# Handing out a bitwise key search on VectorE in two portions per attention unit, and its tie ranking in three pieces

## The chip, the cores and the metric

One core of one Trainium2 chip. The metric is the device time of the kernel in microseconds, median of the runs. Engines: PE is TensorE, DVE is VectorE, ACT is ScalarE, POOL is GpSimd, SP issues the DMAs. Each engine runs its own list of instructions in order, and waits on semaphores for the others.

## The reference

Two transformer blocks in float32, 1024 tokens, width 1024. What matters here is the first block. Its attention has two halves: a dilated window attention (8 heads), and an attention in which each query sees only its top 256 keys by an index score.

```python
q_pos = start + jnp.arange(BLOCK)
causal = key_pos[None, :] <= q_pos[:, None]
dots = jnp.einsum('bqhd,bsd->bqhs', qi_blk, ki).astype(jnp.float32)
score = jnp.einsum('bqh,bqhs->bqs', wi_blk.astype(jnp.float32), jax.nn.relu(dots)) * IDX_SCALE
score = jnp.where(causal[None], score, -jnp.inf)
_, sel = lax.top_k(score, topk)
...
s = jnp.where(valid[:, None], s, -jnp.inf)
p = jax.nn.softmax(s, axis=-1)
return jnp.einsum('bhqk,bqkd->bqhd', p.astype(v.dtype), v_sel)
```

The rest of the first block (gates, output projection, a gated feed-forward part of 2816) and the second block (two kinds of attention, a feed-forward part of 4096) are not touched.

## The kernel before, in words

The kernel first writes a list of stages, `S`, in Python. Every engine's program goes through the same list and emits its own instructions of each stage. So the order of the list is the order on every engine, and a stage that only one engine has (such as `topk`, on DVE alone) takes its place in that engine's queue.

**Units.** Attention of the first block goes by units (phase, head pair c, tile i). Phase a is the dilated half: c = 0 to 3, and for each the tiles i = 0 to 7 of 128 queries. Phase b is the sparse half: the tiles from 0 to 7, and for each the four pairs. Below, a(1,7) is pair 1, tile 7. A unit of tile i has 128 (i + 1) keys, for two heads. For tiles 4 to 7 its scores are made in two passes of at most 512 keys; each pass has a PSUM buffer `big` (there are two). `take` on PE gives a pass the buffer that the woven weight product doesn't hold, and waits until its previous content has been read.

The stages of a unit:

- `sc`: PE multiplies queries and keys (L1090); DVE reads the result with bias and minimum into `prob` (L2123); ACT is left the exponentials (L1430), whose sums go to `sm`.
- `nm`: DVE takes the reciprocals `rc` of the two sums (L2134); ACT scales both rows with them (L1424).
- `pv`: PE transposes the probabilities (L1113), ACT copies them out of PSUM (`pt`, L1384), PE multiplies them with the values (L1128). ACT does the next unit's two exponentials between these copies.
- `oc`: DVE copies the result to `y_a` or `y_b` (L2157).

`attend` runs them with one unit ahead: in step n it puts nm(n), then pv(n-1), sc(n+1), oc(n-1), and then `topk` with the portion of unit n. Between them `weave` puts pieces of weight products on PE (L924): projections in phase a, 16 gates in phase b. For a gate ACT reads PSUM (L1456) and POOL multiplies `gst_b` (L2490); POOL also splits the weights (`w_lo`, L2400) and in phase a rotates queries and keys (L2457, L2460, L2464).

**The search.** The 256th largest index score of each query is found bit by bit, for the tiles 2 to 7 in three batches, (2, 3, 4), (5, 6) and (7). For each of 32 bits there is a *count* per tile (L2059: how many scores reach `edge`) and one *step* per batch (L2065 makes `flip`, L2070 changes `edge`). When a batch is through, each of its tiles has a *rank* piece of seven operations (L2080 to L2093) that writes the mask over the index scores `idx_acc`. All run on DVE. The mask of a tile is wanted by the first b unit of that tile.

Each piece has a planned cost (a count P(i+1)/960 + 0.2, a step 0.75, a ranking 5P(i+1)/960 + 1.2). `spread(s)` is a unit's portion, `share` times its planned PE time; `topk(budget)` adds it to a credit (at most 12) and takes pieces while the credit is more than half the cost of the next one. So what is left over counts in the next call.

Of the kernel before, what the change touches and what calls it, by code (L numbers as in the profile page):

```python
# [22 lines left out]
P = 128  # L23
# [90 lines left out]
def _emit(nc, ctx, known, a):  # L114
    base0 = (nc.sbuf_base + 63) // 64 * 64

    def at(name, offset, shape, dt=F32):
        return nc.alloc_sbuf_tensor_at(name, shape, dt, offset=base0 + offset)
# [26 lines left out]
    edge, above = at("edge", M0 + 7168, [P, QT]), at("above", M0 + 7200, [P, QT])  # L145
# [7 lines left out]
    rot1, rot2 = at("rot1", R0 + 8 * K, [P, T]), at("rot2", R0 + 12 * K, [P, T])  # L153
# [14 lines left out]
    acc_at = [sum(P * (j + 1) for j in range(i)) for i in range(QT + 1)]  # L168
    acc = at("idx_acc", G2 + 46 * K, [P, acc_at[QT]])
# [261 lines left out]
    batches = [(2, 3, 4), (5, 6), (7,)]  # L431
    search = []
    counts = []
    for tiles in batches:
        for bit in range(31, -1, -1):
            counts += [(P * (i + 1) / 960 + 0.2, "count", bit, i, tiles) for i in tiles]
            counts.append((0.75, "step", bit, tiles))
    ranks = [[(5 * P * (i + 1) / 960 + 1.2, "rank", i, tiles) for i in tiles] for tiles in batches]
    credit, share = [0.0], [0.0]

    def take_pieces(wanted):

        n0 = len(search)
        while counts and wanted():
            search.append(counts.pop(0)[1:])
        if len(search) > n0:
            add("topk", n0, len(search))

    def topk(budget):

        def wanted():
            if credit[0] <= counts[0][0] / 2:
                return False
            credit[0] -= counts[0][0]
            return True

        credit[0] = min(credit[0] + budget, 12.0)
        take_pieces(wanted)
# [45 lines left out]
    def attend(units, filler, late, before=None):  # L504

        if before:
            before(units[0])
        add("sc", units[0], 0)
        for n, s in enumerate(units):
            weave_in(filler.get(n, []))  # L510
            add("nm", s, 0)
            if n:
                add("pv", units[n - 1], 0)
                add("pv", units[n - 1], 1)
                weave(group_points(units[n - 1]))
            if n + 1 < len(units):
                if before:
                    before(units[n + 1])
                add("sc", units[n + 1], 0)
            if n:  # L520
                add("oc", units[n - 1])
            if n + 1 < len(units):
                weave(score_points(units[n + 1]))
            for f in late.get(n, []):
                add(*f)
            topk(spread(s))
        return units[-1]

    def attend_pairs(units, filler, early, late):

        add("sc", *units[0])
        for n, (s, ti) in enumerate(units):
            weave_in(filler.get(n, []))
            if n >= 2 and ti == 0 and s[0] == "m":
                add("pt", units[n - 1][0])
            if n + 1 < len(units):
                add("sc", *units[n + 1])
                weave(2)
            for f in early.get(n, []):
                add(*f)  # L540
            add("nm", s, ti)
            if n >= 2:
                old = units[n - 2 + (ti == 0)][0]
                add("pv", old, ti)
                if ti:
                    add("oc", old)
                weave(3 if ti == 0 else 1)
            elif woven:
                add("ahead", 3)
                weave(3)  # L550
            for f in late.get(n, []):
                add(*f)
        return units[-1][0]

    def last_product(s):

# [4 lines left out]
    def spread(s):  # L561

        return share[0] * (0.75 * (s[2] + 1) + 1.36 * (score_points(s) + group_points(s)))
# [22 lines left out]
    for tiles, after in zip(batches[1:], ranks[1:]):  # L586
        n = 1 + max(n for n, x in enumerate(counts) if x[1:] == ("step", 0, tiles))
# [97 lines left out]
    order = []  # L685
# [1126 lines left out]
    def _(dve):  # L1812
# [88 lines left out]
        for stage, *x in S:  # L1901
# [66 lines left out]
            elif stage == "lin" and x[0][:2] != "va":  # L1968
                name, = x
                kind, c = name[:2], name[2:]  # L1970
# [12 lines left out]
            elif stage == "cnorm":  # L1983
                n = {"cq0": 0, "cq1": 1, "ckv": 2}[x[0]]
# [25 lines left out]
            elif stage == "idx":  # L2010
                c, = x
                dve.wait_ge(*s_te.at("t", "wi", 0))
                for hh in range(2):
                    for i in range(2, QT):
# [3 lines left out]
                        z = acc[:, acc_at[i]:acc_at[i + 1]]  # L2018
# [8 lines left out]
            elif stage == "iparts":  # L2027
                c, = x
# [8 lines left out]
            elif stage == "fill":  # L2037
# [4 lines left out]
                for i in range(2, QT):  # L2042
                    z = acc[:, acc_at[i + 1] - P:acc_at[i + 1]]
# [5 lines left out]
            elif stage == "topk":  # L2049
# [3 lines left out]
                for n in range(x[0], x[1]):  # L2053
                    kind, *what = search[n]
                    if kind == "count":
                        bit, i, tiles = what
                        z, tally = acc[:, acc_at[i]:acc_at[i + 1]], (rot1 if n >= late_pieces else tally_a)[:, 0:P * (i + 1)]
                        dve.wait_ge(s_tk.sem, s_tk.count)
                        dve.tensor_scalar(tally, z, edge[:, i:i + 1], 0.0, ALU.is_ge, ALU.add,  # L2059
                                          accum_out=above[:, i:i + 1]).then_inc(*s_tk.mark("count", bit, i))  # L2060
                    elif kind == "step":
                        bit, tiles = what
                        t = slice(tiles[0], tiles[-1] + 1)
                        dve.wait_ge(*s_tk.at("count", bit, tiles[-1]))
                        dve.tensor_scalar(flip[:, t], above[:, t], TOPK - 0.5, float(2 ** bit) if bit < 31 else -1.0, ALU.is_lt,  # L2065
                                          ALU.mult).then_inc(*s_tk.mark("flip", bit, tiles))
                        dve.wait_ge(*s_tk.at("flip", bit, tiles))
                        e = edge[:, t].bitcast(I32)
                        if bit:
                            ins = dve.scalar_tensor_tensor(out=e, in0=flip[:, t], scalar=2 ** (bit - 1), in1=e, op0=ALU.bitwise_xor,  # L2070
                                                           op1=ALU.bitwise_xor)
                        else:
                            ins = dve.tensor_tensor(e, flip[:, t], e, ALU.bitwise_xor)
                        ins.then_inc(*s_tk.mark("step", bit, tiles))
                    else:
                        i, tiles = what
                        z, e = acc[:, acc_at[i]:acc_at[i + 1]], edge[:, i:i + 1]
                        tie, order = rot1[:, 0:P * (i + 1)], rot2[:, 0:P * (i + 1)]
                        dve.wait_ge(s_tk.sem, s_tk.count)
                        dve.tensor_scalar(tie, z, e, 0.0, ALU.is_gt, ALU.add, accum_out=above[:, i:i + 1]).then_inc(*s_tk.mark("above", i))  # L2080
                        dve.wait_ge(*s_tk.at("above", i))
                        dve.tensor_scalar(spare[:, i:i + 1], above[:, i:i + 1], -1.0, float(TOPK), ALU.mult, ALU.add).then_inc(*s_tk.mark("spare", i))
                        dve.tensor_scalar(tie, z, e, None, ALU.is_equal).then_inc(*s_tk.mark("tie", i))
                        dve.wait_ge(*s_tk.at("tie", i))
                        dve.tensor_tensor_scan(order, tie, tie, 0.0, ALU.add, ALU.max).then_inc(*s_tk.mark("order", i))
                        dve.wait_ge(*s_tk.at("order", i))
                        dve.scalar_tensor_tensor(out=tie, in0=order, scalar=spare[:, i:i + 1], in1=tie, op0=ALU.is_gt,
                                                 op1=ALU.mult).then_inc(*s_tk.mark("late", i))
                        dve.wait_ge(*s_tk.at("late", i))
                        dve.scalar_tensor_tensor(out=tie, in0=z, scalar=e, in1=tie, op0=ALU.is_lt,  # L2090
                                                 op1=ALU.add).then_inc(*s_tk.mark("out", i))
                        dve.wait_ge(*s_tk.at("out", i))
                        dve.tensor_scalar(z, tie, MASKED, None, ALU.mult).then_inc(*s_tk.mark("mask", i))  # L2093
                        dve.wait_ge(*s_tk.at("mask", i))
            elif stage == "sc":
                s, ti = x
                st = step_of(s)
                n = nstep[s]
# [11 lines left out]
                for part, (k0, k1) in enumerate(spans):  # L2110
# [4 lines left out]
                    for at_, (lane, i, m) in enumerate(lanes(st, ti)):  # L2115
                        p = st["prob"][m][n % 2][:, lane, k0:k1]
                        c = 4 * (n % 2) + 2 * lane + m
# [8 lines left out]
            elif stage == "nm":  # L2126
                s, unit = x
                st = step_of(s)
                n = nstep[s]
                maps = st["n_maps"]  # L2130
                if st["heads"]:
                    c = 4 * (n % 2)
# [3 lines left out]
                for ti, i, _ in lanes(st, unit)[0:1]:  # L2136
                    nk = keys(st, i)
                    c = 4 * (n % 2) + 2 * ti
# [11 lines left out]
            elif stage == "oc":  # L2150
                s, = x
# [195 lines left out]
            elif stage in ("dnorm", "donorm"):  # L2347
                if stage == "dnorm":
                    which, h = x
                    key, gain, z = ("dnorm", which, h), which, (dqb if which == "dq" else dkb)[h % 2][:, :]  # L2350
                    out = (which, h)
                else:
                    h, = x
                    key, gain, z, out = ("donorm", h), "dout", yd[:, h, :], ("do", h)
# [12 lines left out]
            elif stage == "mn2":  # L2367
# [12 lines left out]
                z = (qz if which == "q" else kz)[h][:, :]  # L2380
# [488 lines left out]
```

## Time and profile before

| | us |
|---|---|
| median of 3 runs | 3199.21 |
| lowest, highest | 3197.5, 3201.7 |
| the profiled execution, its time | 3197.21 |
| its span | 3195.4 |
| PE busy over the span | 2968.6 (93%) |
| DVE busy over the span | 1757.7 (55%) |

Durations and spans below are those of the profiled execution. The attention units and the search lie between 194 and 840 us: phase a until 492, then some projections, phase b from 520. In the rows, times are us from the start of the span, "[x <-Y]" is how long the engine had been idle and whom it waited for, and "mn_part" is the minimum that DVE writes while it reads the first of two passes.

### The profile page before, as it was taken

To read this page: it belongs to the slowest core of one execution; us is meant where nothing else is said; L and a number is where in the kernel's file an instruction comes from. 1 tells how busy PE (TensorE), PEld (TensorE's weight loads), DVE (VectorE), ACT (ScalarE), POOL (GpSimd) and SP (SyncE) were. 2 spreads that over 40 slices of the span, in tenths; PEclk is the share of its full clock that TensorE was granted. 3 is DMA by queue.
4 is the path that set the end of the run, shared out by engine and by line. 5 is a ranking of instruction groups with operands and counts; after the bars stand their busy time and mean duration, and the time that the engine had idled before them with its cause. 6 is when DMAs were issued, how large, how long until landed. Compare 5 with 4: busy or idle time off the path is not lost. (4 is left out here: it accounts for less than half of the span.)

```text
span 3195.4 us, 36533 instructions
## 1 busy us (share of the span) xinstructions
PE 2968.6 (93%) x13886; PEld 2291.0 (72%) x13886; DVE 1757.7 (55%) x2633; ACT 1218.3 (38%) x1810; POOL 1251.4 (39%) x698
## 2 busy tenths in 40 slices
PE   7899887899999999999998899987889999999999
PEld 5666655666778788887886566655777788878887
DVE  4777776775232644445684554575453554455544
ACT  3455543554433433333133344455453322222110
POOL 4324324122244887773246110031002697732221
PEclk8999998999999999999999999998999999999999
DMA  6322111111251223324221311010002233342322
GB/s 176 84 54 60 47 45 48 40 54 44 80 187 52 67 83 92 82 79 138 66 90 35 110 39 33 14 40 17 10 4 89 67 108 105 118 159 92 101 76 73
DMA packets 279311, 236.37 MB, mean 74 GB/s; under 512 B 23748, under 2 KB 251972, under 8 KB 278596
## 3 DMA queue, kind: packets, MB, share of 16 engines
q1 hardware_dynamic: 279176, 234.65, 24.7%
q8 instruction: 75, 1.23, 0.2%
q14 instruction: 60, 0.49, 0.1%
HBM read 171.14 MB, written 53.51 MB: 70 GB/s over the span
## 5 line engine op out<-in xcount | busy, mean ns | idle before, releaser
L924 PE MATMUL big<-g_hi,w_hi 128*128 128x512 f32 x2112 | 693.2, 410 | 40.0 <-POOL w_lo L2400 16.5
L2400 POOL TENSOR_TENSOR w_lo<-w_raw,w_hi 128x1024 fp32r<-128x1024 f32 x147 | 357.2, 2430 | 927.5 <-ACT w_hi L1347 927.5
L924 PE MATMUL big<-g_lo,w_hi 128*128 128x512 f32 x2112 | 662.8, 395 | 0.0
L924 PE MATMUL big<-g_hi,w_lo 128*128 128x512 f32 x2112 | 659.9, 394 | 0.0
L924 PEld LDWEIGHTS big<-g_hi,w_hi 128*128 128x128 f32 x2112 | 381.8, 191 | 197.6 <-issue 121.8
L924 PEld LDWEIGHTS big<-g_lo,w_hi 128*128 128x128 f32 x2112 | 402.0, 191 | 88.4
L924 PEld LDWEIGHTS big<-g_hi,w_lo 128*128 128x128 f32 x2112 | 401.1, 190 | 87.9
L1347 ACT ACTIVATE w_hi<-w_raw 128x1024 fp32r<-128x1024 f32 x147 | 154.7, 1053 | 394.5 <-PE big L924 377.4
L1375 ACT ACTIVATE a_hi<-a_raw 128x512 fp32r<-128x512 f32 x114 | 72.1, 633 | 338.0 <-POOL a_raw L2407 338.0
L1196 PE MATMUL big<-b_hi,a_hi 128*128 128x512 f32 x456 | 178.5, 391 | 8.0 <-DVE b_lo L2204 6.1
L1196 PE MATMUL big<-b_hi,a_lo 128*128 128x512 f32 x456 | 178.1, 391 | 0.0
L1196 PE MATMUL big<-b_lo,a_hi 128*128 128x512 f32 x456 | 178.0, 390 | 0.0
L2415 POOL TENSOR_TENSOR a_lo<-a_raw,a_hi 128x512 fp32r<-128x512 f32 x114 | 153.7, 1348 | 31.9 <-ACT a_hi L1375 31.9
L2216 DVE TENSOR_TENSOR c<-c,big 128x512 f32<-128x512 f32 x114 | 78.3, 687 | 151.4 <-PE big L1196 150.0
L2216 DVE TENSOR_TENSOR c<-c,obank 128x512 f32<-128x512 f32 x76 | 52.2, 687 | 190.0 <-ACT c L1621 180.5
L1384 ACT ACTIVATE pt<-tbank 128x512 f32<-128x512 f32 (+1 forms) x160 | 84.0, 553 | 181.4 <-PE tbank L1113 181.2
L2490 POOL TENSOR_TENSOR gst_b<-gst_b,r_rep 128x1024 f32<-128x1024 f32 x16 | 38.4, 2402 | 243.7 <-ACT gst_b L1456 243.7
L2059 DVE TENSOR_SCALAR_CACHE_REDUCE tally_a<-idx_acc,edge 128x384 f32<-128x384 f32 (+2 forms) x147 | 126.6, 861 | 5.2
L1196 PE MATMUL tbank<-b_hi,a_hi 128*128 128x512 f32 x304 | 119.3, 392 | 4.2 <-POOL a_lo L2415 4.2
L1113 PE MATMUL tbank<-ident_sb,prob 128*128 128x128 f32 x576 | 88.5, 294 | 36.8 <-ACT prob L1424 34.6
L1424 ACT ACTIVATE prob<-prob,rc 128x256 f32<-128x256 f32 (+7 forms) x128 | 92.2, 769 | 79.2 <-DVE rc L2134 79.1
L1196 PE MATMUL tbank<-b_lo,a_hi 128*128 128x512 f32 x304 | 118.3, 389 | 0.0
(337 smaller groups left out, 5570.5 us busy)
## 6 DMA issues: line engine op xcount, KB each, us to landing
a_spill<-c SPq DMA_DIRECT2D x54, 512.0 KB, 3.3
g_lo<-a_spill SPq DMA_DIRECT2D x54, 512.0 KB, 5.1
w_raw<-in_w_in SPq DMA_DIRECT2D x51, 512.0 KB, 4.3
w_raw<-in_w_down SPq DMA_DIRECT2D x40, 512.0 KB, 4.3
w_raw<-in_w_up SPq DMA_DIRECT2D x27, 512.0 KB, 6.0
u_raw<-in_w_up SPq DMA_DIRECT2D x27, 512.0 KB, 6.0
rot<-rope_in SPq DMA_DIRECT2D x68, 128.0 KB, 2.3
g_spill<-gst_b SPq DMA_DIRECT2D x16, 512.0 KB, 3.0
```

The source lines that it names most:

```text
L924: ins = pe.matmul(out[0:m, HALF * h:HALF * h + HALF], w[slot][:, col:col + m], x[:, HALF * h:HALF * h + HALF], start=p == 0, stop=p == tot ...
L1113: ins = pe.transpose(tbank[tn[0] % 2][:, o:o + P], st["prob"][0][n % 2][:, ti, P * kt:P * kt + P], ident[:, :])
L1196: ins = pe.matmul(banks[q], w[q][:, P * k:P * k + P], x[q][:, k, :], start=(k == 0 and z == 0), stop=(k == 3 and z == 2))
L1347: act.activation(w_hi[w % 2][:, :], w_raw[w % 2][:, :], ACT.Copy).then_inc(*s_whi.mark(w))
L1375: act.activation(ah[q][:, :], az[q][:, :] if src is None else src, ACT.Copy).then_inc(*s_ah.mark(stage, q, n))
L1384: act.activation(dest, src, ACT.Copy).then_inc(*s_te.mark(*key))
L1424: act.activation(p, p, ACT.Copy, scale=rc[:, c:c + 1]).then_inc(*s_nrm.mark(s, lane))
L2059: dve.tensor_scalar(tally, z, edge[:, i:i + 1], 0.0, ALU.is_ge, ALU.add, accum_out=above[:, i:i + 1]).then_inc(*s_tk.mark("count", bit, i))
L2216: dve.tensor_tensor(dest, one_, banks[other] if isinstance(other, int) else other, op).then_inc(*s_dr.mark(stage, m, what))
L2400: pool.tensor_tensor(w_lo[s][:, :], w_raw[s][:, :], w_hi[s][:, :].bitcast(F32), ALU.subtract).then_inc(*s_wlo.mark(w))
L2415: pool.tensor_tensor(al[q][:, :], az[q][:, :] if src is None else src, ah[q][:, :].bitcast(F32), ALU.subtract).then_inc(*s_al.mark(stage, ...
L2490: pool.tensor_tensor(z[:, :], z[:, :], r_rep[:, :], ALU.mult).then_inc(*s_gt.mark(name))
```

## The change

In `attend`, the portion of a unit is handed out in two calls. The first comes where the whole one was (behind sc(n+1) and oc(n-1)), and has at most what the two exponentials of the next unit take by a formula, `exponentials`. The rest comes behind the next unit's nm, and so ahead of sc(n+2). The ranking of a tile becomes three pieces, `ties` (three operations), `order` (the scan) and `rank` (the remaining three), which are handed out one by one; their planned costs add up to 6P(i+1)/960 + 1.2.

```diff
-    ranks = [[(5 * P * (i + 1) / 960 + 1.2, "rank", i, tiles) for i in tiles] for tiles in batches]
+    ranks = [[(c * P * (i + 1) / 960 + 0.4, kind, i, tiles) for i in tiles for c, kind in ((1.7, "ties"), (1.8, "order"), (2.5, "rank"))]
+             for tiles in batches]
...
+        rest = 0.0
         add("sc", units[0], 0)
         for n, s in enumerate(units):
             weave_in(filler.get(n, []))
             add("nm", s, 0)
+            topk(rest)
             if n:
                 add("pv", units[n - 1], 0)
...
-            topk(spread(s))
+            first = min(spread(s), exponentials(units[n + 1])) if n + 1 < len(units) else spread(s)
+            rest = spread(s) - first
+            topk(first)
         return units[-1]
...
+    def exponentials(s):
+
+        return 2 * (P * (s[2] + 1) / 960 + 0.25)
...
-                    else:
+                    elif kind == "ties":
                         i, tiles = what
...
                         dve.tensor_scalar(tie, z, e, None, ALU.is_equal).then_inc(*s_tk.mark("tie", i))
+                    elif kind == "order":
+                        i, tiles = what
+                        tie, order = rot1[:, 0:P * (i + 1)], rot2[:, 0:P * (i + 1)]
                         dve.wait_ge(*s_tk.at("tie", i))
                         dve.tensor_tensor_scan(order, tie, tie, 0.0, ALU.add, ALU.max).then_inc(*s_tk.mark("order", i))
+                    else:
+                        i, tiles = what
+                        z, e = acc[:, acc_at[i]:acc_at[i + 1]], edge[:, i:i + 1]
+                        tie, order = rot1[:, 0:P * (i + 1)], rot2[:, 0:P * (i + 1)]
                         dve.wait_ge(*s_tk.at("order", i))
```

## Rows read from the trace of the kernel before

**Rows 1.** Busy time of each engine in three stretches, then PE clock and DMA.

```profile
core 0: us, PE busy (x) PEld busy (x) DVE busy (x) ACT busy (x) POOL busy (x), PEclk, DMA share, GB/s
194.00:482.00 288.00, 260.16 (x1584) 182.37 (x1584) 222.39 (x646) 153.69 (x293) 91.78 (x39) 0.96 0.19 50
482.00:540.00 58.00, 43.46 (x227) 33.64 (x228) 37.58 (x85) 17.92 (x37) 26.88 (x12) 0.85 0.16 38
540.00:840.00 300.00, 279.29 (x1666) 195.64 (x1665) 179.65 (x478) 154.03 (x280) 65.90 (x28) 0.98 0.16 48
```

**Rows 2.** Waits of PE, ACT and DVE, 194 to 840: total us, times, longest.

```profile
PE tbank L1113 <- ACT prob L1424: 34.6, 15, 5.7
PE big L1090 <- DVE mn_part L2123: 9.2, 6, 3.9
...
PE big L1090 <- POOL qb L2464: 5.2, 1, 5.2
...
ACT prob L1424 <- DVE rc L2134: 79.1, 42, 11.2
...
DVE prob L2123 <- PE big L1090: 100.1, 74, 3.8
DVE rc L2134 <- ACT prob L1430: 62.6, 27, 8.4
```

**Rows 3.** Timeline of unit b(2,5): start, duration, instruction, idle before.

```profile
699.53 1.28 DVE L2059 TENSOR_SCALAR_CACHE_REDUCE rot<-idx_acc,edge 128x1024 f32<-128x1024 f32 x1
...
701.04 0.16 DVE L2070 SCALAR_TENSOR_TENSOR edge<-flip,edge 128x1 int32<-128x1 int32 x1
701.24 1.28 DVE L2059 TENSOR_SCALAR_CACHE_REDUCE rot<-idx_acc,edge 128x1024 f32<-128x1024 f32 x1
...
704.01 0.93 ACT L1430 ACTIVATE prob<-prob,mn 128x768 f32<-128x768 f32 x1
...
704.76 1.13 PE L1090 MATMUL big<-kb_b,qb 64*128 64x512 f32 x4
...
705.06 0.17 DVE L2134 RECIPROCAL rc<-sm 128x2 f32<-128x2 f32 x1 [0.46 <-ACT prob L1430]
...
706.02 2.40 POOL L2490 TENSOR_TENSOR gst_b<-gst_b,r_rep 128x1024 f32<-128x1024 f32 x1 [17.43 <-ACT gst_b L1456]
706.04 0.69 DVE L2123 CUSTOM_DVE_ANT_0 prob<-big,idx_acc 128x512 f32<-128x512 f32 x1 [0.81 <-PE big L1090]
...
707.27 0.08 DVE L2123 DVE_READ_ACCUMULATOR2_ANT mn_part<- 128x1 f32 x1
...
707.65 0.70 PE L1090 MATMUL big<-kb_b,qb 64*128 64x256 f32 x4
```

**Rows 4.** Timeline around 748, POOL and DVE.

```profile
748.12 2.40 POOL L2490 TENSOR_TENSOR gst_b<-gst_b,r_rep 128x1024 f32<-128x1024 f32 x1 [14.18 <-ACT gst_b L1456]
...
748.66 1.88 DVE L2070 SCALAR_TENSOR_TENSOR edge<-flip,edge 128x1 int32<-128x1 int32 x1
```

**Rows 5.** Timeline of unit a(1,7).

```profile
326.85 0.19 ACT L1430 ACTIVATION_READ_ACCUMULATOR prob<-prob,mn 128x1 f32 x1
...
331.41 0.16 DVE L2134 RECIPROCAL rc<-sm 128x2 f32<-128x2 f32 x1
...
333.89 1.51 PE L1113 MATMUL tbank<-ident_sb,prob 128*128 128x128 f32 x6 [5.67 <-ACT prob L1424]
```

**Rows 6.** Timeline behind the ranking of tile 7.

```profile
760.98 0.69 DVE L2123 CUSTOM_DVE_ANT_0 prob<-big,idx_acc 128x512 f32<-128x512 f32 x1
...
762.35 0.92 PE L1090 MATMUL big<-kb_b,qb 64*128 64x384 f32 x4 [3.70 <-DVE mn_part L2123]
```

**Rows 7.** Short stretches, columns as in rows 1.

```profile
334.00:337.00 3.00, 3.00 (x12) 2.77 (x13) 2.93 (x5) 2.31 (x5) 2.18 (x1) 0.55 0.00 0
...
257.00:260.00 3.00, 0.83 (x8) 0.67 (x9) 2.34 (x10) 3.00 (x4) 2.37 (x1) 1.00 0.00 0
...
480.00:484.00 4.00, 3.99 (x27) 3.40 (x28) 3.88 (x11) 2.32 (x4) 3.35 (x2) 0.57 0.53 135
...
763.00:767.00 4.00, 4.00 (x15) 3.12 (x14) 1.65 (x6) 0.12 (x1) 0.00 (x0) 0.57 0.00 0
```

## The prediction

> **What bounds the kernel now.** I read the stretch table first. The change acts only from 194 to 840 us, where the attention units and the search run; outside it the order of work is the same. In that stretch PE is busy 260 of 288 us, 43 of 58 and 279 of 300, DVE 222, 38 and 180 [rows 1], so PE is the bound with DVE close behind it in the first half. Then the waits: PE stands 34.6 us, 15 times, for scaled probabilities (ACT prob) and 9.2 us, 6 times, for the first pass of scores being read out of PSUM (DVE mn_part); ACT stands 79.1 us for reciprocals, while DVE stands 62.6 us in front of reciprocals whose exponentials are not done, and 100.1 us in front of score reads whose matmuls are not done [rows 2]. So both directions occur: in some units the search makes the reciprocal late, in others DVE has time to spare.
>
> The timeline of one late unit shows the fault that the edit can mend. The last exponential of unit a(1,7) (phase, head pair, tile) ends at 327.0, but DVE goes on with its portion and divides at 331.41; PE's next transposes wait 5.67 us [rows 5]. The timeline of a usual large unit, b(2,5), shows the other side: the second exponential starts at 704.01 and is done, its sum read, just ahead of the reciprocal at 705.06, PE's first pass of the next scores runs from 704.76 to 705.9, DVE reads it from 706.04 to 707.35, and PE's second pass starts at 707.65 [rows 3]. That second pass takes the PSUM buffer of the first (the other one is held by the woven weight product), so it can't start before the read: 0.3 us of slack, and in most such units under 0.1.
>
> **The change, part by part.** *The split.* A unit's portion is `spread`; the first part becomes what two exponentials take in the planner's formula, 1.6 to 2.6 us for units before tiles 3 to 7 and 0.8 us before tile 0. With share 0.56 the portion is 6 to 8 us for tiles 4 to 7 (0.56 x (0.75 x 6 + 1.36 x 5) = 6.3 for tile 5), so some 4 to 5 us become the remainder, issued behind the next reciprocal and ahead of the next scores. Pieces are whole, and in fact faster than planned: in b a count and its step take 699.53 to 701.24, 1.71 us [rows 3], against 2.02. Counting pieces against the credit gives remainders of 3.1 to 3.9 us in a's tiles 5 and 6, 4.8 to 5.1 in its tile 7, and 2.1 to 4.8 in b's tiles 4 to 6, mostly two counts with their steps (3.4). Tiles below 4 get 0.4 to 2.5.
>
> *What the exponentials really cost.* ACT does the second exponential behind a PSUM read that waits for PE's transposes: the exponentials of b(2,5) are done 5.5 us after DVE's portion starts at 699.53 [rows 3]. In the large units whose portion now just fits, DVE will therefore idle 2 to 3 us ahead of the reciprocal and do the remainder after it.
>
> *The price.* The first score read moves from its present start to the end of the exponentials + 0.2 + remainder. In b(2,5) two counts and two steps give 705.0 + 0.2 + 3.4 = 708.6 instead of 706.04: 2.6 us late, less 0.3 of slack, 2.3 us of PE standing. That such lateness is PE's one to one shows behind the largest ranking: scores read late at 760.98, second pass waits 3.70 [rows 6]. It does not wear off over the units, since each unit's exponentials are tied to PE's own progress. By this sum for each unit, 17 units with a two-pass successor pay: a's tiles 4 to 6 (seven of them) 12 us together, b's tiles 3 to 6 (ten) 18 us: 30 us. Small units have one pass and keep 1 us or more until their transposes: nothing, from 0 to 3 together. Behind tile 7 of a (6.5 us of pieces ahead of the scores of tile 1) the read is 3 us late, covered by the transposes of tile 0; uncovered it would be 3 x 3.
>
> *POOL.* The step's small operation on `edge` takes 0.16 us [rows 3], but 1.88 when it falls in a POOL operation: 748.66 + 1.88 = 750.54, the end of POOL's 748.12 + 2.40 [rows 4]. POOL's gate product starts at 706.02, 0.96 us behind the reciprocal [rows 3], just where the remainder will be, while now the score reads lie there and are not held. A step at 706.9 would wait until 708.4. That hits every second b unit (b(2,4), b(0,5), b(2,5), b(0,6)) for 1.2 to 2.5 us, and in a five units whose rotation runs on POOL: full count 15 us. Where steps fall will shift, so I take half, 8, and keep 0 and 15.
> The Trainium skill, GPSIMD Engine Reference, section 1 (Specifications), says that POOL's SBUF interfaces are shared with VectorE and that instructions with two SBUF inputs or in a 2-port mode contend. The trace agrees, 0.16 against 1.88.
>
> *The gain.* Where the reciprocal was late and PE waited, it comes at the end of the exponentials: PE gets back the smaller of the two. Ten of the 15 waits qualify, for 25 us (from 0.3 at 256.5 to 4.9 at 622.3); one is 4.4 of the 5.67 [rows 5]. Two of these lose 2 to 3.5 us to their own predecessor's remainder, and 1 goes to POOL: 18 stay. The late score reads give 5 of their 9.2 (of the 3.70 about 2, for the ties and order pieces now lie behind the reciprocal) [rows 2, 6]. Gain 23.
>
> *Clock.* After the 5.67 us wait the granted clock is 0.55 over 334 to 337, after a 2.34 us wait 0.57 over 480 to 484, after the 3.70 one 0.57 over 763 to 767, but after a 2.17 us wait 1.00 [rows 7]: the lower level is 1.2 of 2.4 GHz, a half. These rows cost 3 x 0.45 = 1.4 and 4 x 0.43 = 1.7 us; over the nine such stretches between 334 and 767 it is about 2 each. Seven go with their waits (-13), and eight or nine come where the new waits exceed 3 us if POOL holds them up fully (+17), two or three if not (+5). From +4 to -9; I take -3.
>
> *Ranking in three pieces* adds no instruction, and moves them; the planner's total for rankings rises from 5 to 6 units a column, so DVE does about three pieces more before b starts, covered by the wait for the rotated queries (5.2 us on PE [rows 2]), behind which the ties of tile 2 stand too.
>
> Sum: 30 + 8 - 23 - 3 = +12, 30 + 15 - 23 + 4 = +26 with all holds and the clock that goes with them, and 30 - 23 - 9 = -2 without holds. Holds look regular in b, so I go above the middle: +17 on the profiled execution's 3197.2 (span 3195.4), that is 3214. That execution lies 2.0 below the median of the three runs, so the median after is 3216.
>
> **Rivals.**
> 1. *The remainder is hidden* (faster). PE's second pass doesn't suffer, because the read gets done under the woven product. It decides at a mean stall of (23 + 9) / 17 = 1.9 us per unit without holds; at half my stalls, 15, the sum is 15 - 23 - 9 = -17: 3182. For it: 62.6 us of DVE idle before reciprocals are still there and 100.1 before score reads [rows 2]. Against: slack under 0.1 us in front of the second pass, and [rows 6].
> 2. *A wash.* No holds at POOL and no new clock losses: -2, 3197; within 0.2%.
> 3. *POOL holds every step that meets it*, at either end of the remainder: +26 or more, 3225 to 3234. For it: the held step [rows 4] and POOL's place behind the reciprocal [rows 3]. The Trainium skill, GPSIMD Engine Reference, section 1, would have it so.
> 4. *The edit does little*, since credit carries over and whole pieces blur the split. Against: the portion exceeds the exponentials in every unit of both phases. 3199.
> The Trainium skill, TensorE: Matmul & The Clock Gate, Part 1, says that recent activity sets the clock and the throttled state is the default. By that rule the removed long waits return clock and the new short ones may not cost any, rival 2's side; the rows show both outcomes at 2.17 and 2.34 us.
>
> **How the numbers follow.** Forecast (3206 to 3224) 0.45; rival 3, 0.25; rivals 2 and 4, 0.17; rival 1, 0.13. The range 3192 to 3232 leaves 0.1 on each side or less; the forecast's own is 3206 to 3224. A measurement of this kernel tells about 0.2% (6.4 us) from no change: faster 0.13, same 0.17, slower 0.70.
>
> **What would show it.** Right: PE's wait for ACT prob falls from 34.6 to about 13, its wait for DVE mn_part rises from 9.2 to 35 or more, in some 17 portions of 1 to 5 us; DVE idles more than 62.6 us before reciprocals and far less than 100.1 before score reads; PE's busy time in 194 to 840 is nearly unchanged; steps of about 2 us behind reciprocals in b. Wrong, if mn_part stays under 20, or if the second passes wait and the unit still keeps its length, which would mean that PE had slack in these units that I did not see.

## The result, and the profile after

| | before, us | after, us |
|---|---|---|
| median | 3198.88 (4 runs, 3197.5 to 3201.7) | 3237.26 (4 runs, 3235.05 to 3242.92) |
| span of the profiled execution | 3195.4 | 3233.3 |
| first score matmul of phase a to last copy to `y_b` | 666.7 (195.0 to 861.7) | 701.0 (195.3 to 896.3) |
| PE busy over the span | 2968.6 | 2986.5 |

The ratio is 1.0122 [1.0104, 1.0139]: slower by 1.2%, where 3216 (3192 to 3232) was forecast. Of the 37.9 us that the profiled execution's span grew, 34.3 lie between the first scores of phase a and the end of phase b; I call this stretch the attention below. The page's head:

```profile
span 3233.3 us, 36529 instructions
PE 2986.5 (92%) x13886; PEld 2302.1 (71%) x13886; DVE 1746.2 (54%) x2633; ACT 1219.2 (38%) x1810; POOL 1250.0 (39%) x698
```

The waits of PE, ACT and DVE, 194 to 875 us of the kernel after (engine, line, whom it waited for: total us, times, longest), against [rows 2]:

```profile
DVE rc L2150 <- ACT prob L1439: 158.3, 51, 7.9
DVE prob L2139 <- PE big L1099: 50.7, 48, 3.5
PE big L1099 <- DVE mn_part L2139: 46.4, 19, 4.4
ACT prob L1433 <- DVE rc L2150: 17.5, 37, 6.5
ACT prob L1439 <- DVE mn L2139: 15.1, 10, 3.4
PE obank L1137 <- ACT pt L1393: 15.4, 17, 3.6
PE tbank L1122 <- ACT prob L1433: 10.6, 9, 3.2
PE big L1099 <- POOL qb L2480: 3.4, 1, 3.4
```

The rows show an exchange. The reciprocal isn't late any more: ACT waits for it 17.5 us instead of 79.1, and DVE stands 158.3 us in front of reciprocals instead of 62.6. PE gets back 24.0 us of its wait for scaled probabilities. What DVE no longer does before the reciprocal it does before the score read: its idle time there falls from 100.1 to 50.7, and PE's second pass waits 46.4 us, 19 times, instead of 9.2. Over the whole attention all listed waits of PE grow from 64.0 to 83.1 us, by 19.1: +37.2 for `mn_part`, -24.0 for ACT prob, +6.9 for `pt` (9.5 before, 16.4 after), and -1.0 for the others. That is half of the 37.9.

The three longest waits for `pt` (3.59, 2.45 and 2.13 us) come from the late score reads too, by way of ACT. ACT stands 15.1 us for the minimum `mn` of the finished scores, in front of its exponentials; before it was little:

```profile
ACT prob L1430 <- DVE mn L2123: 1.3, 2, 0.7
```

The longest of the three, with the copy of `pt` queued on ACT behind such an exponential (in front of the other two ACT stood 2.23 and 1.91 us for `mn`):

```profile
342.34 1.15 ACT L1439 ACTIVATE prob<-prob,mn 128x1024 f32<-128x1024 f32 x1 [3.37 <-DVE mn L2139]
...
343.49 0.58 ACT L1393 ACTIVATE pt<-tbank 128x512 f32<-128x512 f32 x1
...
344.12 1.12 PE L1137 MATMUL obank<-pt,va 128*64 128x128 f32 x8 [3.59 <-ACT pt L1393]
```

The other half is in the busy time. The same stretches as [rows 1] (busy us and instructions of PE, PEld, DVE, ACT, POOL, then PE clock, DMA share, GB/s):

```profile
core 0: us, PE busy (x) PEld busy (x) DVE busy (x) ACT busy (x) POOL busy (x), PEclk, DMA share, GB/s
194.00:508.00 314.00, 273.39 (x1615) 190.27 (x1615) 219.20 (x659) 157.98 (x300) 94.98 (x41) 0.93 0.18 46
508.00:560.00 52.00, 41.14 (x199) 31.79 (x198) 32.76 (x78) 14.48 (x32) 23.40 (x10) 0.86 0.17 41
560.00:875.00 315.00, 284.19 (x1666) 199.68 (x1665) 177.43 (x474) 153.96 (x277) 67.56 (x28) 0.96 0.15 46
```

PE does the same matmuls (3480 records against 3477), but is busy 598.7 us with them instead of 582.9, and its clock in phase a is 0.93 instead of 0.96. To size this I cut the trace into windows of half a us and summed PE busy x (1 - granted clock) from 197 us to the last copy to `y_b`: before 18.5 us in 9 stretches at the lower level, after 35.0 us in 17. So 19.1 of waits and 16.5 of clock make 35.6, against the 34.3 by which the attention grew. Where the clock fell:

```profile
254.00:258.00 4.00, 3.98 (x9) 2.09 (x10) 1.84 (x6) 0.00 (x0) 0.00 (x0) 0.50 0.17 53
...
705.00:709.00 4.00, 4.00 (x16) 3.37 (x16) 2.82 (x10) 0.94 (x2) 0.23 (x1) 0.58 0.50 138
736.00:740.00 4.00, 4.00 (x16) 3.42 (x15) 2.49 (x8) 1.33 (x3) 0.00 (x0) 0.57 0.10 29
...
722.00:725.00 3.00, 3.00 (x19) 2.58 (x18) 2.69 (x10) 1.30 (x3) 0.00 (x0) 1.00 0.00 0
```

These stand behind waits for `mn_part` of 4.4, 2.1, 3.5 and (the last row) 3.1 us. In the first three rows (0.50 to 0.58) PE is busy all the time, and its instructions take nearly twice as long, as the transposes below show.

The unit of [rows 3], b(2,5), in the kernel after:

```profile
728.35 1.13 PE L1099 MATMUL big<-kb_b,qb 64*128 64x512 f32 x4
728.66 0.17 DVE L2150 RECIPROCAL rc<-sm 128x2 f32<-128x2 f32 x1 [3.86 <-ACT prob L1439]
728.91 0.16 DVE L2079 SCALAR_TENSOR_TENSOR edge<-flip,edge 128x1 int32<-128x1 int32 x1
729.11 1.28 DVE L2068 TENSOR_SCALAR_CACHE_REDUCE rot<-idx_acc,edge 128x1024 f32<-128x1024 f32 x1
729.62 2.39 POOL L2506 TENSOR_TENSOR gst_b<-gst_b,r_rep 128x1024 f32<-128x1024 f32 x1 [24.39 <-ACT gst_b L1465]
730.62 1.42 DVE L2079 SCALAR_TENSOR_TENSOR edge<-flip,edge 128x1 int32<-128x1 int32 x1
732.07 1.28 DVE L2068 TENSOR_SCALAR_CACHE_REDUCE rot<-idx_acc,edge 128x1024 f32<-128x1024 f32 x1
733.39 0.69 DVE L2139 CUSTOM_DVE_ANT_0 prob<-big,idx_acc 128x512 f32<-128x512 f32 x1
734.61 0.08 DVE L2139 DVE_READ_ACCUMULATOR2_ANT mn_part<- 128x1 f32 x1
734.75 0.70 PE L1099 MATMUL big<-kb_b,qb 64*128 64x256 f32 x4 [3.46 <-DVE mn_part L2139]
737.33 1.91 PE L1122 MATMUL tbank<-ident_sb,prob 128*128 128x128 f32 x8
```

Everything of the forecast stands here in order. DVE idles 3.86 us for the sums, then does two steps and two counts. The second step takes 1.42 us instead of 0.16, because it meets POOL's gate product (729.62 + 2.39 = 732.01; 730.62 + 1.42 = 732.04). The score read comes 4.73 us behind the reciprocal instead of 0.98, the second pass waits 3.46 us, and the eight transposes behind it take 1.91 us at half the clock. In the kernel before they took 1.04:

```profile
709.77 1.04 PE L1113 MATMUL tbank<-ident_sb,prob 128*128 128x128 f32 x8
```

### The profile page after: what moved, and what is told of

Read it like the earlier page. It is cut to its first block and busy times, and to the rows that moved or that the text cites. A ratio compares the mean times of both kernels' runs of the same rounds, so it can differ in the third digit from the quotient of the medians.

```text
span 3233.3 us, 36529 instructions
## 1 busy us (share of the span) xinstructions
PE 2986.5 (92%) x13886; PEld 2302.1 (71%) x13886; DVE 1746.2 (54%) x2633; ACT 1219.2 (38%) x1810; POOL 1250.0 (39%) x698
## 5 line engine op out<-in xcount | busy, mean ns | idle before, releaser
L2431 POOL TENSOR_TENSOR a_lo<-a_raw,a_hi 128x512 fp32r<-128x512 f32 x114 | 153.3, 1345 | 31.9 <-ACT a_hi L1384 31.9
L1205 PE MATMUL tbank<-b_hi,a_lo 128*128 128x512 f32 x304 | 118.9, 391 | 0.0
L1205 PE MATMUL obank<-b_hi,a_hi 128*128 128x512 f32 x304 | 118.3, 389 | 0.0
```

The lines of the kernel that those rows point to most:

```text
L1205: ins = pe.matmul(banks[q], w[q][:, P * k:P * k + P], x[q][:, k, :], start=(k == 0 and z == 0), stop=(k == 3 and z == 2))
L2431: pool.tensor_tensor(al[q][:, :], az[q][:, :] if src is None else src, ah[q][:, :].bitcast(F32), ALU.subtract).then_inc(*s_al.mark(stage, ...
```

## The experiments

"Attention" is the stretch defined above, in the profiled execution; ratios are to the kernel before on the same chip, whose median was 3203.53 (e1 to e4), 3204.45 (e5 to e8) and 3203.06 (e9 to e12). "Waits" are PE's for `mn_part` / ACT prob; "lost" is the sum of PE busy x (1 - clock), as above, from 197 us to the last copy to `y_b` (in e1, whose attention starts at 200.5, 1.0 of it lies ahead). Attention, waits and lost are those of one execution each, the ratio is from all runs. The parts outside the attention, where nothing was changed, differ by up to 5.5 us each between executions, so the ratio and the attention say more than the span.

| run | ratio [95%] | span | attention | waits, us | lost, us |
|---|---|---|---|---|---|
| before | | 3195.4 | 666.7 | 9.2 / 34.6 | 18.5 |
| after | 1.0122 [1.0104, 1.0139] | 3233.3 | 701.0 | 46.4 / 10.6 | 35.0 |
| e1_ranks_only | 0.9929 [0.991, 0.9948] | 3189.9 | 650.5 | 7.6 / 21.6 | 19.8 |
| e2_split_only | 1.0159 [1.0134, 1.0183] | 3242.4 | 710.3 | 49.7 / 9.7 | 31.9 |
| e3_cap15 | 0.9931 [0.9912, 0.995] | 3178.9 | 646.0 | 9.6 / 17.4 | 14.9 |
| e12_cap30 | 1.0061 [1.0044, 1.0079] | 3222.0 | 689.3 | 37.1 / 13.5 | 30.7 |
| e4_small_gates | 1.0072 [1.0047, 1.0097] | 3227.1 | 694.4 | 40.5 / 10.9 | 34.2 |
| e8_before_small_gates | 0.9979 [0.9967, 0.9991] | 3192.6 | 664.3 | 7.5 / 31.8 | 23.1 |
| e5_pad2 | 1.0054 [1.0037, 1.0071] | 3215.5 | 683.9 | 23.3 / 34.7 | 21.2 |
| e6_pad4 | 1.0224 [1.0207, 1.0241] | 3276.8 | 743.6 | 59.4 / 32.8 | 48.5 |
| e7_weave2 | 1.0025 [1.0016, 1.0035] | 3202.2 | 672.3 | 18.0 / 9.7 | 23.4 |
| e9_cap15_weave2 | 0.994 [0.9926, 0.9955] | 3185.6 | 652.7 | 5.5 / 15.7 | 17.8 |
| e10_ranks_only_weave2 | 0.9967 [0.9954, 0.998] | 3190.3 | 661.8 | 5.4 / 20.6 | 18.3 |
| e11_before_weave2 | 1.0027 [1.0016, 1.0038] | 3211.0 | 680.3 | 8.2 / 31.9 | 24.2 |

### The two halves apart

e1 keeps the ranking in three pieces and hands out the portion whole; e2 keeps the rank piece whole, at its old cost, and splits the portion.

```diff
 # e1_ranks_only, against the kernel after
-            topk(rest)
...
-            first = min(spread(s), exponentials(units[n + 1])) if n + 1 < len(units) else spread(s)
-            rest = spread(s) - first
-            topk(first)
+            topk(spread(s))
 # e2_split_only, against the kernel before
+            topk(rest)
...
-            topk(spread(s))
+            first = min(spread(s), exponentials(units[n + 1])) if n + 1 < len(units) else spread(s)
+            rest = spread(s) - first
+            topk(first)
```

> The ranking in three pieces with its new planned costs, the portion whole as before (no remainder behind the reciprocal). Theory A (the remainder in front of the first score read causes the whole loss): PE's wait for DVE mn_part falls back from 46.4 us to 5 to 12 us, stretches at the lower clock level from 17 to about 8, time 3182 to 3199 us; the smaller pieces make the reciprocals of phase b less late, so PE's wait for ACT prob is 18 to 32 us. Rival B (the costlier planned ranking, which makes portions larger and moves search into phase a, carries a good part of the loss): 3207 us or more.

> The two portions, with the ranking of a tile as one piece at its old cost. Theory A: as slow as the full change or slower, 3232 to 3250 us, with PE's wait for DVE mn_part at 40 to 55 us, since a whole ranking can now fall behind a reciprocal. Rival B: most of the loss goes, 3215 us or less.

Measured: the two halves have opposite signs. The new ranking alone makes the kernel faster by 0.7%, the split alone makes it slower by 1.6%, a little more than expected (median 3253, expected to 3250). The waits of PE in e1, 194 to 890 us:

```profile
PE tbank L1119 <- ACT prob L1430: 21.6, 10, 5.9
PE obank L1134 <- ACT pt L1390: 10.2, 19, 1.0
PE big L1096 <- DVE mn_part L2136: 7.6, 6, 3.7
```

Smaller pieces and a higher planned cost of rankings come together in e1, and no run tells them apart; with both, fewer reciprocals are late. ACT prob falls by 13.0 us, and the wait for `mn_part` hardly changes (9.2 to 7.6). The attention is 16.2 us shorter. The span shows only 5.5 of it: this execution came 5.5 us late into the attention (first scores at 200.48), with a clock of 0.89 over the first 194 us instead of 0.93, and took 5.2 us longer behind it. It is the longest of its six; by the ratio the gain is 23 us.

In e2 PE's wait for `mn_part` is 49.7 us in 18 waits, as in the kernel after. The split is the harm. The new ranking may take a part of it back: 1.0159 against 1.0122, with intervals that overlap.

### The size of the remainder

```diff
 # e3_cap15, against the kernel after (e12_cap30: the same with 3.0)
-            rest = spread(s) - first
-            topk(first)
+            rest = min(spread(s) - first, 1.5)
+            topk(spread(s) - rest)
```

> The full change, but the remainder has at most 1.5 us of planned work and the rest goes in front of the reciprocal. Theory A with a threshold (a remainder costs nothing until it exceeds the time between the reciprocal and the end of PE's first score pass, mostly 1.0 to 1.7 us in large units): one piece fits, PE waits for DVE mn_part 8 to 20 us, for ACT prob 18 to 28 us, time 3180 to 3202 us. Rival C (anything behind the reciprocal delays PE one to one): mn_part 25 us or more, 3210 to 3225 us.

> The full change with the remainder capped at 3.0 us of planned work (mostly one count with its step and at times two counts). Theory E in its new form (waits of 2 us and more lose the clock, shorter ones mostly not): PE's wait for DVE mn_part 15 to 28 us, most single waits under 2 us, stretches at the lower clock level 9 to 13, time 3188 to 3212 us, and the time above the capped version of 1.5 us equals the waits and the lower clock added up to within 4 us. Rival (any remainder of two pieces costs as the full one): 3220 us or more.

With at most 1.5 us behind the reciprocal (in b mostly one count) the split costs nothing: 0.9931, the same as without it. PE's waits over the attention fall from 64.0 us before to 47.3, and the clock loss by 3.6; together 20.3 of the 20.7 us by which the attention is shorter. A unit of b in e3:

```profile
701.16 0.17 DVE L2150 RECIPROCAL rc<-sm 128x2 f32<-128x2 f32 x1 [2.87 <-ACT prob L1439]
701.24 1.26 DVE L2068 TENSOR_SCALAR_CACHE_REDUCE rot<-idx_acc,edge 128x1024 f32<-128x1024 f32 x1
...
701.49 1.13 PE L1099 MATMUL big<-kb_b,qb 64*128 64x512 f32 x4
702.78 0.69 DVE L2139 CUSTOM_DVE_ANT_0 prob<-big,idx_acc 128x512 f32<-128x512 f32 x1 [0.27 <-PE big L1099]
...
704.14 0.92 PE L1099 MATMUL big<-kb_b,qb 64*128 64x384 f32 x4
```

The count fills the time in which PE makes the first pass, and DVE still waits 0.27 us for it; no wait of matmuls is noted before the second pass. That hole is what is free behind a reciprocal. At 3.0 it is overrun: 37.1 us of waits for `mn_part` (15 to 28 were expected) and 0.6% slower than before, 3222.6 us, where 3188 to 3212 was expected. From 1.5 to 3.0 PE's waits grow by 28.5 us (27.5 of them for `mn_part`) and the clock loss by 15.8, together 44.3, and the attention by 43.3. By the ratios two thirds of the harm of the full remainder is there at 3.0 (1.3 of 1.9%).

### The price of a late score read by itself

In the kernel before, 2 or 4 more counts of 1024 columns stand behind the reciprocal of the 16 units of b that have a successor with two passes. Nothing else is changed, and the gain is left out.

```diff
 # e5_pad2 (e6_pad4: 4), behind the reciprocal at L2134 of the kernel before
+                    if s[0] == "b" and s[2] >= 4 or s == ("b", 3, 3, 0):
+                        for k in range(2 if s != b_steps[-1] else 0):
+                            dve.wait_ge(s_tk.sem, s_tk.count)
+                            dve.tensor_scalar(rot1[:, :], acc[:, acc_at[7]:acc_at[8]], edge[:, 0:1], 0.0, ALU.is_ge, ALU.add,
+                                              accum_out=above[:, 0:1]).then_inc(*s_tk.mark("pad", s, k))
```

> The kernel before, with two more counts of 1024 columns (2.8 us, result unused) behind each reciprocal of the 16 units of phase b whose successor has tile 4 or more; no portion is split. It prices a late score read by itself. From the present times between reciprocal and score read (0.2 to 3.6 us) PE's wait for DVE mn_part should rise by 16 to 22 us. Theory E (waits well under 3 us mostly leave the clock alone): 0 to 3 more stretches at the lower clock level, 3215 to 3227 us. Rival F (the clock goes with any such wait): 8 or more such stretches, 3230 us or more. Rival G (PE catches up): mn_part up, but under 3208 us.

> The same with four counts (5.6 us) in each of the 16 places. PE's wait for DVE mn_part rises by 50 to 62 us. Theory E: waits of 3 to 5.5 us lose the clock nearly every time, 11 to 15 stretches more at 1.4 to 2.5 us each, so that the time rises by 20 to 35 us more than the waits: 3270 to 3295 us. Rival G: the time rises by no more than the waits, 3250 to 3262 us.

PE's waits for `mn_part` in e5 (194 to 890) and in e6 (194 to 930):

```profile
PE big L1090 <- DVE mn_part L2123: 23.3, 15, 6.2
```

```profile
PE big L1090 <- DVE mn_part L2123: 59.4, 20, 7.2
```

e5: the wait grows by 14.1 us (16 to 22 were expected) and the clock loss by 21.2 - 18.5 = 2.7; the sum is 16.8, and the attention is 17.2 longer (17.3 by the ratio; the other 2.9 of the span's 20.1 lie outside). e6: 50.2 - 1.8 (ACT prob) + 30.0 = 78.4, and the attention is 76.9 longer (71.8 by the ratio). PE's late reads are therefore in its time one to one, and clock comes on top: a us of such waiting cost 17.2 / 14.1 = 1.2 us in e5 and 76.9 / 48.4 = 1.6 us in e6. The first 2.8 us of extra work behind each reciprocal raised PE's wait by 0.9 us a unit (14.1 / 16), so about 1.9 of them were free, which agrees with e3; with the clock they cost 1.1 (17.2 / 16), and the next 2.8 cost 3.7 (59.7 / 16).

### POOL's hold

The gate product of POOL is done on 8 columns instead of 1024, in the kernel after (e4) and before (e8); the gates are therefore not those of the reference.

```diff
-                pool.tensor_tensor(z[:, :], z[:, :], r_rep[:, :], ALU.mult).then_inc(*s_gt.mark(name))
+                n = 8 if stage == "gate" else T
+                pool.tensor_tensor(z[:, 0:n], z[:, 0:n], r_rep[:, 0:n], ALU.mult).then_inc(*s_gt.mark(name))
```

> The full change, with POOL's gate product done on 8 of 1024 columns (2.4 us of POOL work per gate left out, 16 gates; the other columns stay unscaled). Theory D (a step of the search that meets POOL is held until POOL is through, and this is in every second large unit of phase b): PE's wait for DVE mn_part falls by 4 to 9 us, two to four stretches at the lower clock level go, time 3221 to 3231 us. Rival (POOL plays no part, two counts and two steps explain the stalls): within 3 us of the full change, 3234 to 3240 us.

> Control of the run with POOL's gate product on 8 columns: the same edit in the kernel before. Theory D (POOL hurts the full change because its product lies behind the reciprocal, where the remainder is): no change here beyond 6 us, 3193 to 3201 us. Rival (the gate product costs the attention units whatever the order of the search): 8 us or more faster, 3191 us or less.

The same place of b(2,5) in e4: the reciprocal is at 726.96, the product takes 0.20 us and ends during the first count of the remainder. The second step, held for 1.42 us in the kernel after, takes 0.16, and PE's second pass waits 2.18 us instead of 3.46.

```profile
727.92 0.20 POOL L2507 TENSOR_TENSOR gst_b<-gst_b,r_rep 128x8 f32<-128x8 f32 x1 [23.12 <-ACT gst_b L1465]
728.92 0.16 DVE L2079 SCALAR_TENSOR_TENSOR edge<-flip,edge 128x1 int32<-128x1 int32 x1
...
731.79 0.70 PE L1099 MATMUL big<-kb_b,qb 64*128 64x256 f32 x4 [2.18 <-DVE mn_part L2139]
```

The wait for `mn_part` falls by 5.9 us, the attention by 6.6, the ratio from 1.0122 to 1.0072 (on two chips). The same edit is worth 0.2% on the kernel before, 7 us by the ratio, where no change beyond 6 was expected; so the part of the split's harm that is due to this product's holds is about 0.3% of 3200, some 9 us by the ratios, whose intervals together leave as much open, and 6.6 - 2.4 = 4 by the attention. It is seen in the rows of b(2,5), and it is a small term: 40.5 us of waits stay without it. Two to four stretches at the lower clock were expected to go; the loss fell only from 35.0 to 34.2. The waits that got shorter, 2.18 us here and 1.83 in b(0,6), still had half clock behind them.

The edit doesn't take away every hold. The operations of the steps (`flip` and `edge`) that took over 0.3 us instead of the usual 0.16 lost 33.9 us together over the attention of the kernel after and 26.3 in e4, where the holds by POOL's other work, `v_f` and the rotation among it, remain. In the kernel before it was 38.7: the split added none in sum, and put some of them in front of a score read.

### Cover for the late read

PE is given two pieces of woven matmuls instead of one between the first and the second pass of scores, in the kernel after (e7), in e3 (e9), in e1 (e10) and in the kernel before (e11).

```diff
-                    weave()
+                    weave(2 if part == 0 and len(parts_of_row(s, ti)) == 2 and kind in "ab" else 1)
```

> The full change, with PE taking six passes' worth of the woven product (2.8 us) instead of three (1.4 us) between the two score passes of a unit of the first block; the sum of woven work is the same, so later places of the unit get less. Theory A: the second pass has 1.4 us more cover, PE's wait for DVE mn_part falls from 46 to 22 to 32 us and most stretches at the lower clock level behind it go, but what is taken early is missing while PE waits for ACT later (pt, prob up by 5 to 15 us): 3205 to 3228 us. Rival H (PE has no work to spare, so the wait only moves): 3233 us or more.

> The remainder capped at 1.5 us of planned work, ranking in three pieces, and the longer woven cover between two score passes. Theory A: the 9.6 us of waits for DVE mn_part that the cap left fall to 2 to 5 us and one to three stretches at the lower clock level go; 3168 to 3180 us. Rival I (the cover only moves waits to ACT's PSUM copies): 3180 to 3190 us.

> No remainder, ranking in three pieces, and the longer cover. Theory A: 7.6 us of waits for DVE mn_part fall to 2 to 4 us, PE's 21.6 us for ACT prob stay; 3171 to 3181 us, a few us above the capped version with the same cover. Rival I: 3180 us or more.

> The longer cover alone, in the kernel before. Theory A: of 9.2 us of waits for DVE mn_part 3 to 6 go, and up to two of the nine stretches at the lower clock level; 3190 to 3198 us. Rival I: 3198 to 3206 us.

With the split, the cover takes the wait for `mn_part` from 46.4 to 18.0 us and the loss by clock from 35.0 to 23.4; the kernel is at 1.0025 instead of 1.0122. So PE's standing at that place carried most of the harm. Where there is nothing to cover the same edit costs: 0.27% on the kernel before, 0.4% on e1, about 0.1% on e3, within the intervals. All three had been expected to gain by theory A (3190 to 3198, 3171 to 3181 and 3168 to 3180 us), and came out at 3211, 3194 and 3186; rival I has the last two, and e11 lies above both. PE's waits in e7:

```profile
PE obank L1137 <- ACT pt L1393: 21.3, 28, 3.6
PE big L1099 <- DVE mn_part L2139: 18.0, 15, 5.0
```

The pieces that stand between the passes are missing elsewhere, among others in front of the value products: over the attention the wait for `pt` rises from 16.4 to 21.3 here, and in e11 from 9.5 to 14.9. In e11 PE also waits 4.4 us more for `rope_in` and 3.5 more for `gst_b`, which ACT reads out of PSUM; all waits together grow by 8.6 us and the clock loss by 5.7, which covers the 13.6 us by which e11's attention grew.

## Why the prediction was right and wrong

**Direction and place: right.** The split moves search pieces from ahead of the reciprocal, where in most units they were hidden or late by little, to ahead of the score read, where PE has under 0.1 us of slack. e2 shows the harm with the split alone, and e5 and e6 show it with the late read alone. The signs named beforehand came as said: ACT prob 10.6 ("about 13"), `mn_part` 46.4 in 19 waits ("35 or more, in some 17"), DVE idle 158.3 before reciprocals and 50.7 before score reads.

**The clock: the step that failed.** The prediction took -3 us for it. "Seven go with their waits (-13), and eight or nine come where the new waits exceed 3 us if POOL holds them up fully (+17), two or three if not (+5). From +4 to -9; I take -3." Measured: +16.5. The gate product's holds weren't the reason: e4 is without them and still loses 34.2 us to the clock. (The low end is a slip as well: -13 + 5 is -8.) Two things were wrong. The first is the assumption that only waits over 3 us cost clock. In the kernel after, 17 of the 18 waits of PE from 2.0 us up are followed by half clock (for instance 2.14 us at 704, [rows 7] had one of 2.17 that was not), and none of the seven between 1.4 and 1.8 us is. The new waits lie mostly from 2 to 4 us. I had one row at 2.17 with full clock and one at 2.34 with half, and put the border far above both. Over all fourteen traces, within 4 us of the wait's end, 158 of 170 waits from 2.0 us up are followed by half clock, and 8 of 52 between 1.4 and 2.0: no length decides alone. "About 2 each" was right: 18.5 / 9 before and 35.0 / 17 after are both 2.06 us. The number was wrong, 8 stretches more instead of one or two fewer. With 2.0 as the border about half of my 17 stalls (38 / 17 = 2.2 us in the mean) would have had one, an estimate of 17 - 13 = +4. The second thing lies beyond that: which waits there would be, and how long. Of the 17 waits with half clock behind them ten are for `mn_part`, six over 3 us and four from 2.0 to 2.8. In phase a the waits for `mn_part` are 20.9 us instead of 5.1, where 12 had been added; one of them is 3.77, in a(2,5). The other seven are for something else: three for `pt` (3.59, 2.13 and 2.45 us), which weren't counted at all, two for ACT prob, and one each for `mn` and `qb`. With the clock term PE's busy time failed too: forecast nearly unchanged, it rose by 15.8 us.

The range ended at 3232, and its largest sum at +26, because its clock term ended at +4. The upper end should have been a stretch for each of the 17 stalls, 17 x 2 - 13 = +21, since no row excluded that; the sum would have been +43 and would have held the measured +38.

The Trainium skill, TensorE: Matmul & The Clock Gate, Part 1, says that how busy TensorE has been recently sets its clock. The rows agree in that the clock fell behind waits. The use that I made of it, that the new short waits may cost none, is refuted by the rows (2.14 us at 704, half clock from 705).

**POOL's holds: too small.** "Where steps fall will shift, so I take half, 8, and keep 0 and 15." In b(2,5) a step is held, 1.42 us; in a(0,6) one is held for 2.27 us and the second pass waits 4.41. For b(2,5) the prediction has a stall of 2.3 us without a hold, and holds of 1.2 us or more on top; 3.46 was measured, and 2.18 in e4. In b(0,6) it is 3.43 against 1.83. There the full holds came, as rival 3 had it. The Trainium skill, GPSIMD Engine Reference, section 1 (Specifications), says that the two engines share SBUF interfaces, with contention for VectorE instructions in a 2-port mode or with two SBUF inputs. The trace agrees for the operation on `edge`, which reads `flip` and `edge` and took 1.42 us instead of 0.16. In waits alone this changes little: without the clock the forecast was 30 + 8 - 23 = 15 and with all holds 22, and 19.1 was measured. By e4 and e8 the gate product's holds are worth 4 to 9 us, with as much uncertainty.

**Stalls and gain: right in sum.** 38 - 23 = 15 against 19.1. The difference is less than what the wait for `pt` brought, +6.9, which I hadn't counted. The rows at 342 to 344 show the way of its longest wait: a late score read makes ACT's exponential late, and with it the copy behind it.

**Ranking in three pieces: wrong.** It was costed at nothing ("adds no instruction, and moves them"). e1 shows a gain of 0.7%, with 13.0 of ACT prob's 34.6 us. This also splits the gain: of the 24.0 us that ACT prob fell, 13.0 would have come without the split. Beside e1 the split had only 11.0 us left to earn, for 38.8 us of waits for `mn_part` and 15.2 of clock.

**Rivals.** Rival 1 (hidden) fell with e5: work behind the reciprocal beyond about 1.9 us isn't hidden. It holds for remainders up to that size, which is e3. Rivals 2 and 4 fell with the result. Rival 3 had the holds right in the two units named above; most of the excess over 3224 is the clock, which e4 keeps.

The fastest are e1 (0.9929) and e3 (0.9931). Their intervals overlap, so a small remainder wins nothing that can be measured over none; the simpler one is to keep the portion whole and rank in three pieces.

**Open.** Why the wait of 3.10 us at 721 in the kernel after kept full clock (722 to 725, above). Whether e1's gain comes from the smaller pieces or from the higher planned cost. Whether cap 1.5 is the best size: nothing below 1.5 or between 1.5 and 3.0 was run.

## What to carry to other kernels

Work that can wait is put behind a dependency by the hole that the timeline shows there (here the 1.1 us of PE's first pass and what lies around it), not by the length of the operation that it makes room for; what overruns the hole is late for the next reader, and here that reader holds a PSUM buffer that PE wants. A change that exchanges a few long stalls of PE for many of 2 to 4 us is costed with the clock: here each us of added waiting made the attention 1.2 us (e5), 1.6 us (e6) or 1.8 us (34.3 / 19.1, the change itself) longer. And the size and planned cost of the pieces can be worth more than where they are put: a change with two parts is costed, and tried, as two.

## What the runs showed of the hardware

- TensorE fell to half clock behind short waits inside an otherwise busy stretch: 17 of 18 waits of 2.0 to 4.4 us in the kernel after, none of seven from 1.4 to 1.8 us. The stretches lost 1.4 to 4.3 us each, in both kernels. The exceptions are 3.10 us with full clock behind it, and before 2.17 us with full clock [rows 7]. In all fourteen traces it was 158 of 170 waits from 2.0 us up, and 8 of 52 between 1.4 and 2.0 (one of 1.83 us in e4).
- The step on one to three int32 columns, 0.16 us by itself, was held until POOL's product ended: 1.42 us at 730.62, and 2.27 us in a(0,6), with PE's wait of 4.41 us behind it. The small operation before it, which makes `flip`, was held too: 1.58 us instead of 0.15 to 0.17, until POOL's product was through (335.35 + 2.37 = 337.72):

```profile
246.93 2.27 DVE L2079 SCALAR_TENSOR_TENSOR edge<-flip,edge 128x3 int32<-128x3 int32 x1
...
254.02 2.08 PE L1099 MATMUL big<-ka,qa 64*128 64x512 f32 x4 [4.41 <-DVE mn_part L2139]
...
335.35 2.37 POOL L2506 TENSOR_TENSOR v_f<-v_f,r_rep 128x1024 f32<-128x1024 f32 x1 [10.16 <-ACT v_f L1471]
...
336.16 1.58 DVE L2074 TENSOR_SCALAR flip<-above 128x3 int32<-128x3 f32 x1
```

  Counts with an accumulated sum (1.28 us at 729.11 and 732.07), of which the first overlaps the same POOL product, kept their time.
